# A two-layer streaming encoder: the first weight unit in quarters between the x tiles, its first two pieces multiplied row pair by row pair

## The reference

```python
def rms_norm(x, g):
    xf = x.astype(jnp.float32)
    y = xf * lax.rsqrt(jnp.mean(xf * xf, axis=-1, keepdims=True) + EPS)
    return (y * g.astype(jnp.float32)).astype(x.dtype)

def swiglu(x, w_in, w_out):
    gate, up = jnp.split(x @ w_in, 2, axis=-1)
    return (jax.nn.silu(gate) * up) @ w_out

def half_ffn(x, g, w_in, w_out):
    return x + FFN_RES * swiglu(rms_norm(x, g), w_in, w_out)
```

## Time and profile before

| | |
|---|---|
| median of 3 runs | 1118.63 us (1117.05, 1118.63, 1118.66) |
| span of the profiled execution, first to last instruction | 1116.9 us; what lies around the span is not shown |
| TensorE busy | 1099.2 us, 98% |
| VectorE, ScalarE, GpSimd busy | 63%, 46%, 11% |
| DMA | 172.04 MB moved, mean 154 GB/s |

### The profile page before, as it was taken

The page is one execution under the profiler, slowest core; times in us unless marked ns, Lnnn a source line. Parts: engine busy times, 40 slices in busy tenths (PEclk is TensorE's granted clock), DMA queues, the critical chain, the costliest instruction groups (busy, mean ns, idle before and its releaser), DMA issues.

```text
span 1116.9 us, 21215 instructions
## 1 busy us (share of the span) xinstructions
PE 1099.2 (98%) x8113; PEld 1075.8 (96%) x8113; DVE 707.9 (63%) x1073; ACT 510.8 (46%) x760; POOL 126.0 (11%) x159
## 2 busy tenths in 40 slices
PE   8999999999999999999999999999999999999996
PEld 7999999998999999999999999999988899999996
DVE  7766665564665866666546666645599776666442
ACT  6444443354454544444335444433466554444331
POOL 3000001100002600000120000011142410000011
PEclk9999999999999999999999999999999999999998
DMA  6544454432332654445434544543332244444531
GB/s 235 188 172 166 153 204 156 151 107 102 127 123 89 216 188 150 172 180 184 179 113 154 182 153 156 204 176 141 113 142 97 82 172 162 173 165 178 182 129 43
DMA packets 24203, 172.04 MB, mean 154 GB/s; under 512 B 3248, under 2 KB 3536, under 8 KB 5600
## 3 DMA queue, kind: packets, MB, share of 16 engines
q1 hardware_dynamic: 21888, 167.16, 41.6%
q0 software_dynamic: 960, 2.23, 0.6%
q10 hardware_dynamic: 1312, 2.07, 0.5%
HBM read 168.88 MB, written 2.56 MB: 153 GB/s over the span
## 4 chain that ended last, share of the span: by engine, by line
PE 93%; DVE 3%; ACT 2%; DMA 1%; issue 1%; POOL 0%; DVEq 0%; ACTq 0%; SPq 0%
PE acc L360 30%; PE acc L362 29%; PE acc L361 29%; DVE wlo L347 1%; DMA raw<-in_w 1%; DVE rstd L946 1%; PE mb L595 0%; ACT whi L340 0%; PE mb L614 0%; PE mb L529 0%; PE num L521 0%; PE acc L642 0%; ACT work L867 0%; PE mb L387 0%; PE num L524 0%
## 5 line engine op out<-in xcount | busy, mean ns | idle before, releaser
L360 PE MATMUL acc<-xhi,whi 128*128 128x288 f32 x1696 | 508.1, 300 | 3.3 <-DVE xlo L941 2.8
L340 ACT ACTIVATE whi<-raw 128x1024 fp32r<-128x1024 f32 (+1 forms) x292 | 328.8, 1128 | 390.1 <-PE acc L362 373.7
L361 PE MATMUL acc<-xlo,whi 128*128 128x288 f32 x1696 | 502.3, 296 | 0.0
L362 PE MATMUL acc<-xhi,wlo 128*128 128x288 f32 x1696 | 500.5, 295 | 0.0
L347 DVE TENSOR_TENSOR wlo<-raw,whi 128x1024 fp32r<-128x1024 f32 (+1 forms) x292 | 389.2, 1333 | 158.7 <-ACT whi L340 148.7
L360 PEld LDWEIGHTS acc<-xhi,whi 128*128 128x128 f32 x1696 | 319.6, 188 | 7.2 <-issue 4.5
L362 PEld LDWEIGHTS acc<-xhi,wlo 128*128 128x128 f32 x1696 | 321.3, 189 | 0.0
L361 PEld LDWEIGHTS acc<-xlo,whi 128*128 128x128 f32 x1696 | 320.4, 189 | 0.5
L360 PE MATMUL acc<-ahi,whi 128*128 128x288 f32 x832 | 247.1, 297 | 0.9 <-DVE alo L1179 0.7
L361 PE MATMUL acc<-alo,whi 128*128 128x288 f32 x832 | 245.4, 295 | 0.0
L362 PE MATMUL acc<-ahi,wlo 128*128 128x288 f32 x832 | 244.6, 294 | 0.0
(11 more groups left out here) (208 smaller groups left out, 618.4 us busy)
## 6 DMA issues: line engine op xcount, KB each, us to landing
raw<-in_w SPq DMA_DIRECT2D x113, 1024.0 KB, 4.8
raw<-in_w SPq DMA_DIRECT2D x32, 1408.0 KB, 5.8
x<-in_xT SPq DMA_DIRECT2D x4, 288.0 KB, 5.8
raw<-in_w SPq DMA_DIRECT2D x2, 512.0 KB, 5.2
out_yT<-x ACTq DMA_DIRECT2D x3, 288.0 KB, 2.3
work<-in_cst POOLq DMA_DIRECT2D x1, 560.0 KB, 4.0
work<-in_c ACTq DMA_DIRECT2D x1, 514.0 KB
out_cp<-work POOLq DMA_DIRECT2D x4, 128.5 KB, 2.4
```

Source lines behind the costliest of these rows:

```text
L340: act.activation(dst, src, ACT.Copy).then_inc(hi_done, 1)
L360: pe.matmul(out, wh, hi[:, k, :], start=(first and n == 0), stop=False)
L361: pe.matmul(out, wh, lo[:, k, :], start=False, stop=False)
L362: mm = pe.matmul(out, wl, hi[:, k, :], start=False, stop=(last and n == len(tiles) - 1))
```

## The change

Unit 0 is loaded in four quarters of 512 columns, each with its own semaphore: quarters 0 and 1 are the first and second four row blocks of piece 0, quarters 2 and 3 those of piece 1. The loads run x pair 0, quarters 0 and 2, x pair 1, quarter 1, x pair 2, quarter 3, x pair 3, unit 1. ScalarE and VectorE split a quarter ahead of each x pair, in the order 0, 2, 1, 3. ScalarE's squares of tiles 1, 3, 5 and 7 come behind x tile 5, behind x tile 7, behind the split of piece 2 and behind that of piece 3; the load of the constants is issued behind x tile 7. TensorE runs 18 warm-ups, multiplies pieces 0 and 1 by pairs of row blocks in turn (`very_first`), and sums `ssq` behind piece 2, not ahead of it. Only the first stage is touched.

```diff
--- before.py
+++ after.py
@@ -34,8 +34,9 @@
 EPS = 1e-6
 BIG, TINY = 1e30, 1e-30
 Y_POOL = 6
-WARM_UP = 16
+WARM_UP = 18
 RAW = 2 * (KF // 2)
+QUARTER = KD // 2 * P
 TOK = [(0, 128), (128, 128), (256, 32)]


@@ -211,7 +212,8 @@
         landed = [sem("landed0"), sem("landed1")]
         x_in = [sem(f"x_in{i}") for i in range(KD // 2)]
         chain_d, chain_a = sem("vector_chain"), sem("scalar_chain")
-        first_in = sem("first_in")
+        first_in = [sem(f"first_in{n}") for n in range(4)]
+        head_hi, head_lo = sem("head_hi"), sem("head_lo")
         hi_done = sem("hi_done")
         lo_done = sem("lo_done")
         piece_done = sem("piece_done")
@@ -303,13 +305,23 @@
                 sp.dma_start(dst, src).then_inc(landed[u % 2], 16)


-            half = TILES[0] * P
-            for n in range(KD // 2):
-                if n == 0:
-                    sp.dma_start(raw[:, 0, 0:half], a["w0"][0][:, 0:half]).then_inc(first_in, 16)
-                if n == 2:
-                    sp.dma_start(raw[:, 0, half:2 * half], a["w0"][0][:, half:2 * half]).then_inc(landed[0], 16)
+            def quarter(n):
+
+                sp.dma_start(raw[:, 0, n * QUARTER:(n + 1) * QUARTER], a["w0"][0][:, n * QUARTER:(n + 1) * QUARTER])\
+                    .then_inc(first_in[n], 16)
+
+            def load_x(n):
+
                 sp.dma_start(x[:, 2 * n:2 * n + 2, :], a["xT"][:, 2 * n:2 * n + 2, :]).then_inc(x_in[n], 16)
+
+            load_x(0)
+            quarter(0)
+            quarter(2)
+            load_x(1)
+            quarter(1)
+            load_x(2)
+            quarter(3)
+            load_x(3)
             for i, (kind, units, _, L) in enumerate(STAGES):
                 src = a[f"w{i}"]
                 u0 = FIRST_UNIT[i]
@@ -329,15 +341,29 @@

         def split_hi(act, it, c, L):

-            if c == 0 and isinstance(it, int):
-                act.wait_ge(first_in, 16)
-            else:
-                act.wait_ge(landed[(c // 2) % 2], 16 * it + 16 * (c // 4 + 1))
+            act.wait_ge(landed[(c // 2) % 2], 16 * it + 16 * (c // 4 + 1) - (16 if (c // 2) % 2 == 0 else 0))
             if c >= 4:
                 act.wait_ge(piece_done, 4 * it + c - 3)
             src = raw[:, (c // 2) % 2, (c % 2) * L * P:(c % 2 + 1) * L * P]
             dst = whi[:, c % 4, 0:L, :].rearrange("p a b -> p (a b)")
             act.activation(dst, src, ACT.Copy).then_inc(hi_done, 1)
+
+        def head_split_hi(act, n):
+
+            act.wait_ge(first_in[n], 16)
+            dst = whi[:, n // 2, (n % 2) * 4:(n % 2) * 4 + 4, :].rearrange("p a b -> p (a b)")
+            act.activation(dst, raw[:, 0, n * QUARTER:(n + 1) * QUARTER], ACT.Copy).then_inc(hi_done if n % 2 else head_hi, 1)
+
+        def head_split_lo(dve, n):
+
+            if n % 2:
+                dve.wait_ge(hi_done, n // 2 + 1)
+            else:
+                dve.wait_ge(head_hi, n // 2 + 1)
+            hi = whi[:, n // 2, (n % 2) * 4:(n % 2) * 4 + 4, :].rearrange("p a b -> p (a b)").bitcast(F32)
+            dst = wlo[:, n // 2, (n % 2) * 4:(n % 2) * 4 + 4, :].rearrange("p a b -> p (a b)")
+            dve.tensor_tensor(dst, raw[:, 0, n * QUARTER:(n + 1) * QUARTER], hi, ALU.subtract)\
+                .then_inc(lo_done if n % 2 else head_lo, 1)

         def split_lo(dve, it, c, L):
             dve.wait_ge(hi_done, 4 * it + c + 1)
@@ -412,11 +438,30 @@
                 ss_sum()
                 norm_no[0] += 1

+            def very_first():
+
+                for k in range(0, KD, 2):
+                    for q in range(2):
+                        if k == 0:
+                            pe.wait_ge(head_lo, q + 1)
+                        if k == KD // 2:
+                            pe.wait_ge(lo_done, q + 1)
+                        mm = products(pe, group_bank(q), q, [(k, k), (k + 1, k + 1)], xhi, xlo,
+                                      k == 0, k == KD - 2, before=x_ready if q == 0 else None)
+                        if k == KD - 2:
+                            mm.then_inc(piece_done, 1)
+
             def ffn_in(i):
                 c0_, G0 = 2 * FIRST_UNIT[i], FIRST_GROUP[i]
-                first_two(i, c0_, G0)
+                if i == 0:
+                    very_first()
+                else:
+                    first_two(i, c0_, G0)
                 for q in range(2, 4):
                     in_piece(i, 0, c0_ + q, q, G0 + q)
+                    if i == 0 and q == 2:
+                        ss_sum()
+                        norm_no[0] += 1
                 with pe.Fori(1, KF // 2) as it:
                     for q in range(4):
                         in_piece(i, it, c0_ + q, q, G0 + q)
@@ -882,18 +927,25 @@


             act.dma_start(norms[:, :, :], a["norms"]).then_inc(norms_in, 16)
-            split_hi(act, 0, 0, 8)
-            act.wait_ge(norms_in, 16)
+            def head_square(m):
+
+                act.activation(x_squares[:, m // 2, :], x[:, m, :], ACT.Square).then_inc(x_sq, 1)
+
             for m in range(KD):
-                if m == 4:
-                    act.dma_start(cst[:, :], a["cst"][:, 0:3 * P]).then_inc(cst_in, 16)
-                    split_hi(act, 0, 1, 8)
+                if m % 2 == 0:
+                    head_split_hi(act, (0, 2, 1, 3)[m // 2])
+                if m == 0:
+                    act.wait_ge(norms_in, 16)
                 act.wait_ge(x_in[m // 2], 16)
                 hi_of_x(m, N_F1)
-                if m % 2 == 1:
-                    act.activation(x_squares[:, m // 2, :], x[:, m, :], ACT.Square).then_inc(x_sq, 1)
+                if m == 5:
+                    head_square(1)
+            act.dma_start(cst[:, :], a["cst"][:, 0:3 * P]).then_inc(cst_in, 16)
+            head_square(3)
             split_hi(act, 0, 2, 8)
+            head_square(5)
             split_hi(act, 0, 3, 8)
+            head_square(7)
             act.dma_start(graw[:, :, :], a["w_gates"]).then_inc(par_in, 16)
             act.dma_start(bg[:, :], a["b_gates"]).then_inc(par_in, 16)
             act.dma_start(m0[:, :], a["m0"]).then_inc(par_in, 16)
@@ -1233,11 +1285,10 @@
             dve.memset(epst[:, :], EPS).then_inc(const_done, 1)
             dve.memset(ghi[:, :, :].bitcast(F32), 0.0).then_inc(g_zero, 1)
             dve.memset(glo[:, :, :].bitcast(F32), 0.0).then_inc(g_zero, 1)
-            split_lo(dve, 0, 0, 8)
             dve.wait_ge(norms_in, 16)
             for m in range(KD):
-                if m == 4:
-                    split_lo(dve, 0, 1, 8)
+                if m % 2 == 0:
+                    head_split_lo(dve, (0, 2, 1, 3)[m // 2])
                 dve.wait_ge(x_in[m // 2], 16)
                 lo_of_x(m, N_F1, m + 1)
             split_lo(dve, 0, 2, 8)
```

## The result

The changed kernel takes 1120.72 us (median of 12 runs, 1119.21 to 1123.41), the kernel before 1118.88 (12 runs, 1116.91 to 1119.68): ratio 1.0020, 95% interval 1.0011 to 1.0030. The forecast was 1115.4 us, with a range up to 1117.3. Runs of one kernel spread by more than the first three did: the kernel before lies between 1115.69 and 1122.65 in 35 runs taken later.

What follows compares the result with a forecast made beforehand. TensorE, busy for 98% of the span, was taken as the bound. Piece 2 done at 18.6 to 19.9, wait to 20.0, sum 0.48, weights 0.15, piece 3 3.2: 23.8 against 27.0; 1118.63 - 3.2 = 1115.4, range 1113.0 to 1117.3.

Steps and rivals of the forecast that it cites:

- Loads: Head loads: smaller rows cost nothing; quarter 1 lands at 7.5, x pair 3 at 9.7, first square starts at 9.4.
- GpSimd's chain: Norm's squares and adds in the head: ten operations take 10.1 us, begun at 9.8, ended at 19.9.
- The upper bound, 11.0: GpSimd's ten operations: 11.0 us if they meet two long subtractions and not one, ending at 20.8.
- The price of one collision: GpSimd operation beside a long VectorE subtraction: 0.8 us extra, from 1.66 against 0.82.
- the rival with the small chance: Head, clock stays down: all 96 matmuls at 0.24, 3.8 us slower, 1122.4; chance 0.05.
- the known fall: Clock fall at 256.4 to 259.8 us, granted 0.51, cited as following a stretch of four-row matmuls.
- VectorE's low parts of x: Head: near 0.52 us each up to about 10 us and near 1 behind it.
- The first two pieces: TensorE in the head: end at 15.4 to 16.7 as the clock rises at 11.3 or 14.0; before, 20.12.
- a sign of being wrong that the prediction names: TensorE in the head: stops between row pairs would show operands coming late; none expected before piece 2's end.
- given back at piece 4: Unit 2 lands at 18.5, not 16.5, delaying piece 4: gain 1.9 to 2.9, about 1116.2; chance 0.10.
- The square-root, reciprocal and evacuation chain: Before piece 4: first evacuation 3.0 us behind std's start, just hidden by piece 3's 3.2.
- what the prediction said in the head: Head: piece 3 done at 23.8 against 27.0, a gain of 3.2 us.

Runs made afterwards that it cites:

- e2: Changed kernel with each quarter of unit 0 contiguous in device memory, nothing else different; median 1120.05 us, ratio to before 1.0006.
- e6: Changed kernel with VectorE's low part of piece 4 moved behind the reciprocal; one run only, no ratio given, piece 4 starts at 27.59 us.
- e12: Changed kernel with 20 matmuls on zeros between piece 2 and the norm's sum; 1118.86 us, ratio to before 1.0006.
- e5: Changed kernel with squares behind each odd x tile and quarters contiguous in memory; median 1121.49 us, ratio to before 1.0027.
- e4: Changed kernel with the squares of tiles 2, 4 and 6 left out of the first norm's sum; 1117.09 us, ratio to before 0.9983.
- e8: Changed kernel with contiguous quarters and ScalarE squaring tiles 1 to 7, GpSimd multiplying once and adding; median 1117.19 us, ratio to before 0.9985.
- e10: Kernel of e8 with the parameter loads moved from ScalarE to SyncE behind unit 3; 1116.85 us, ratio to before 0.9980.
- e3: Changed kernel with the norm's sum on TensorE behind piece 3 and not piece 2; median 1122.35 us, ratio to before 1.0030.
- e11: Changed kernel with ScalarE squaring tiles 1 to 7, quarters still cut from 8192-byte rows; ratio to before 0.9986.
- e7: Kernel before with 18 warm-up matmuls in place of 16, nothing else; 1119.07 us, ratio to before 1.0003.
- e9: Kernel of e5 with the mixer's six parameter loads moved from ScalarE to SyncE behind unit 3; ratio to before 1.0001.

## Why the prediction was wrong

**Loads: the step that failed first.** "Smaller rows I cost at nothing, because x tiles with rows close to the quarters' (2304 bytes to 2048) land at this rate." In the trace of before those x tiles travelled among halves of a unit with 4096-byte rows. In the new mix, with 2048-byte rows cut out of 8192-byte ones, the queue ran at 249 to 305 GB/s. Quarter 1 landed at 9.45, 1.9 us late, and the first square started at 11.05, not 9.4: 1.65 us. e2 shows the cause: the same sizes from contiguous memory land 0.3 to 0.5 us behind the forecast, and the first square starts at 9.73. Why rows of 2048 bytes at this pitch are slow where the x tiles' 2304 bytes are not was not tried.

**GpSimd's chain: 10.1 us forecast, 11.6 measured.** The upper bound, 11.0, counted two long subtractions. There were three collisions: pieces 2 and 3 are subtracted back to back beside two operations, and piece 4's subtraction, which came behind the chain before, lies beside a third. The prediction didn't count that one, though its own times put it there: unit 2 at 16.5 and a split of 1.06 bring piece 4's subtraction to about 17.6, inside a chain of 9.8 to 19.9. The lateness of the loads isn't the reason, since e2 has the same three with an earlier chain. e6 takes out the third alone. The price of one collision was right (1.65 against 0.67 to 0.82): 10.1 and two more at 0.8 make 11.7. The two errors together, 1.65 + 1.5, are nearly the whole of 23.39 against 20.0.

**The clock: the rival with the small chance.** The prediction wrote against the slower rival that the known fall "followed a stretch of four-row matmuls, not a stop of 1 us". The stop was 3.32 us, since it grew with the sum's lateness, and the fall came. The rival had it too large, though: 13 matmuls ran slowly, not 96, and the price was 1.4 us. With the stop filled, e12 has no fall there and starts piece 4 1.67 us earlier; in one execution, that shows the stop to be the cause. So forecast and result go together: -3.2 + 1.65 + 1.5 + 1.4 gives +1.35, measured at piece 4 +1.65.

**What held.** VectorE's low parts of x took 0.51 to 0.52 us up to 11.8 us and 0.92 and 1.06 behind it. The first two pieces ended at 16.2 (15.4 to 16.7 forecast) and piece 2 at 19.9, the upper end of 18.6 to 19.9. This was not for the reasons given, and so luck: real work began at 6.58, not 7.2, and the clock rose at 7.4, not at 11.3, while stops of 0.28 to 0.66 us on late operands between the row pairs, a sign of being wrong that the prediction names, took that gain back. The rival "given back at piece 4" did not happen here (split of piece 4 at 17.98, table loaded at 20.3, evacuation at 26.68), but it did in e5. The square-root, reciprocal and evacuation chain took 3.0 us, as forecast, and was hidden.

**With the sum on time** the changed order is worth what the prediction said in the head: e4 and e8 start piece 4 3.3 and 4.0 us earlier than before. Of that, the runs keep 0.0017 and 0.0015 of 1118.8, 1.9 us (0.3 to 3.6) and 1.7 us (0.1 to 3.1). In the profiled executions the rest goes with the half-clock stretches further on. That of e8 has one near 250 us, as before has the earlier trace rows, and its span is 4.0 us shorter, which is all of its gain in the head. That of e10 has none, and its span is 5.0 us shorter with 3.6 gained in the head. The two rows are e8's stretch and e10 from 20 us almost to the end, with a mean granted clock of 1.00:

```profile
252.70:256.10 3.40, 3.40 (x14) 2.93 (x13) 2.23 (x9) 0.00 (x0) 0.00 (x0) 0.50 0.51 210
```

```profile
20.00:1100.00 1080.00, 1077.09 (x8014) 1055.99 (x8012) 684.88 (x1049) 496.74 (x737) 113.77 (x142) 1.00 0.43 153
```

That of e4 has three such lengths, and its span is only 0.3 shorter with 3.3 gained in the head. So each length costs from 1.4 us (e10) to about 1.75 (the changed kernel, 3.4 longer with 1.65 lost in the head). More of them in the other runs would explain what the medians lack, but of those runs there is no trace.

## What to carry to other kernels

Where a reduction stands between two stretches of TensorE's work, move its inputs forward with the work, or leave it: bringing the matmuls forward and the squares back made a stop of 3.3 us, and the fall of the clock behind it cost 1.4 more. When a step is moved, price its collisions at its new place, where its neighbours are others, and let one lateness run on into the next term of the sum. Cut a load into pieces that lie contiguous in HBM, and check what another queue has ahead of the next one.

## What the hardware showed unexpectedly

- A stop can cost more than its length. With stops of 3.07 to 3.41 us the granted clock fell to the 1.2 GHz level for 3.4 or 6.8 us, within the stop (e2, e3, e5) or 1.1 us after its end (changed); with 0.71 to 2.34 us before the sum (e6, e8, e10, e11, e12) it did not. In e7 it fell 0.65 us after the end of the stop of 2.46 us behind the warm-ups, and in e9 behind stops of 0.68 us at most, so the length of a stop alone doesn't decide it.
- Up to the first rise the record shows a granted 1.00 though matmuls start 0.24 us apart; in the head the spacing is to be read.
- Parameters of 930 KB in six loads, asked for by another engine up to 2.3 us ahead, made a 1 MB load take 8.4 us (e5) instead of 4.7 (e9).
